# Four of the weight units per attention stage are reduced by GpSimd, and TensorE only adds their partitions

## The reference

```
# hybrid_layer, run for l = 0 and l = 1
shift, scale, gate = split(c @ w_ada[l] + b_ada[l], 3)       # [1024] @ [1024, 3072]
u = x * (1 + scale) + shift
h = split_cols(u @ w_in[l])
... attention of three kinds (dsa, fox, nsa: compressed, selected, window) ...
y = (mix * silu(h["gate"])) @ w_out[l]
x = layer_norm(ALPHA * x + (1 + gate) * y, ln_g[l], ln_b[l])

# second_block, once
mod   = silu(c_2)     @ w_mod_2 + b_mod_2                    # [1024] @ [1024, 6144]
mod_c = silu(c_ctx_2) @ w_mod_2 + b_mod_2
sh1, sc1, gt1, sh2, sc2, gt2       = split(mod, 6)
csh1, csc1, cgt1, csh2, csc2, cgt2 = split(mod_c, 6)
... gated delta net on latents and context, then 16 experts, uses of the context end early ...
```

## Time and profile before

| | us |
|---|---|
| three runs: lowest, median, highest | 1301.52, 1306.74, 1315.82 |
| the profiled execution, whole | 1302.77 |
| its span in the trace | 1301.0 |
| TensorE busy | 1073.4 (83%) |
| VectorE busy | 430.2 (33%) |
| ScalarE busy | 225.9 (17%) |
| GpSimd busy | 64.3 (5%) |

### The profile page before, as it was taken

The page is one execution under the profiler, slowest core; times in us unless marked ns, Lnnn a source line. Parts: engine busy times, 40 slices in busy tenths (PEclk is TensorE's granted clock), DMA queues, the critical chain, the costliest instruction groups (busy, mean ns, idle before and its releaser), DMA issues.

```text
span 1301.0 us, 17728 instructions
## 1 busy us (share of the span) xinstructions
PE 1073.4 (83%) x7534; PEld 576.8 (44%) x7534; DVE 430.2 (33%) x1039; ACT 225.9 (17%) x550; POOL 64.3 (5%) x73
## 2 busy tenths in 40 slices
PE   2899999999999999999998879677766666666675
PEld 0344674444576448975777865322211111111111
DVE  0124656333765545354256673311000000000001
ACT  0102125111213423532121232100000000000001
POOL 1001000000100000002203400000000000000000
PEclk9899999999999999899988999798887878888879
DMA  9663337553346962113110016189999999999996
GB/s 375 288 265 123 130 129 283 185 197 130 129 146 258 428 241 109 65 57 139 66 66 3 3 66 228 63 363 431 429 428 430 430 430 429 430 430 429 431 429 260
DMA packets 24558, 323.66 MB, mean 249 GB/s; under 512 B 2736, under 2 KB 2736, under 8 KB 5152
## 3 DMA queue, kind: packets, MB, share of 16 engines
q1 hardware_dynamic: 22448, 314.18, 58.9%
q0 software_dynamic: 2032, 8.35, 1.9%
HBM read 321.47 MB, written 1.05 MB: 248 GB/s over the span
## 4 chain that ended last, share of the span: by engine, by line
PE 58%; DMA 29%; DVE 7%; issue 3%; ACT 1%; another core or an unknown queue 1%; SPq 0%; POOL 0%; DVEq 0%; ACTq 0%; POOLq 0%
PE banks L602 48%; DMA Vt_to_O<-in_stream 14%; DMA ring<-in_stream 10%; PE banks L613 3%; DMA QKT<-in_stream 2%; DMA zuv_to_Kt<-in_stream 2%; PE banks L2039 1%; PE banks L826 1%; DVE Vt_to_O L2309 1%; PE banks L847 1%; PE banks L812 1%; PE banks L809 1%; PE banks L713 1%; DVE probs L1163 1%
## 5 line engine op out<-in xcount | busy, mean ns | idle before, releaser
L602 PE MATMUL banks<-ring,uT 128*128 128x512 f32 (+1 forms) x512 | 225.0, 595 | 6.3 <-DVE uT L1022 3.7
L602 PEld LDWEIGHTS banks<-ring,uT 128*128 128x128 f32 x512 | 96.4, 192 | 119.7 <-issue 114.0
L602 PE MATMUL banks<-ring,scr 128*32 128x512 f32 (+1 forms) x656 | 112.8, 696 | 38.8 <-DMA ring<-in_stream 38.5
L602 PE MATMUL banks<-ring,UWK 128*32 128x512 f32 (+1 forms) x368 | 91.4, 786 | 15.1 <-DMA ring<-in_stream 10.5
L2506 DVE SCALAR_TENSOR_TENSOR UWK<-UWK,banks 128x256 f32<-128x256 f32 x16 | 6.7, 422 | 285.5 <-ACT UWK L2750 285.5
L602 PE MATMUL banks<-scr 64*64 64x64 f32 (+2 forms) x2048 | 82.4, 234 | 6.3 <-DVE scr L2357 5.2
L602 PEld LDWEIGHTS banks<-scr 64*64 64x64 f32 (+1 forms) x2048 | 79.0, 144 | 12.3 <-DVE scr L2357 5.8
L602 PEld LDWEIGHTS banks<-ring,scr 128*32 128x32 f32 (+1 forms) x656 | 29.7, 127 | 114.7 <-DMA ring<-in_stream 60.5
L2039 PE MATMUL banks<-UWK 128*128 128x512 f32 x128 | 58.7, 602 | 25.6 <-DVE UWK L2516 25.6
L613 PE MATMUL banks<-ring,KC 128*32 128x512 f32 x384 | 53.1, 683 | 27.1 <-DMA ring<-in_stream 27.1
L2750 ACT ACTIVATE UWK<-banks 128x256 f32<-128x256 f32 x16 | 6.1, 383 | 397.7 <-PE banks L602 397.7
(11 more groups left out here) (361 smaller groups left out, 1191.7 us busy)
## 6 DMA issues: line engine op xcount, KB each, us to landing
ring<-in_stream SPq DMA_DIRECT2D x106, 2048.0 KB, 17.3
QKT<-in_stream SPq DMA_DIRECT2D x14, 2048.0 KB, 30.8
Vt_to_O<-in_stream SPq DMA_DIRECT2D x14, 2048.0 KB, 30.8
zuv_to_Kt<-in_stream SPq DMA_DIRECT2D x14, 2048.0 KB, 30.1
w<-in_w POOLq DMA_DIRECT2D x2, 1024.0 KB, 9.6
probs<-in_rows POOLq DMA_DIRECT2D x4, 512.0 KB, 4.7
const<-in_consts SPq DMA_DIRECT2D x1, 1215.0 KB, 5.6
resid<-in_x SPq DMA_DIRECT2D x1, 1024.0 KB, 24.2
```

The lines of the kernel that those rows point to most:

```text
L602: return pe.matmul(o, a, b, start=start, stop=stop)
```

## The change

In each of the two attention stages GpSimd takes four units: of layer 0's stage the units 0 to 3 of the six of `w_ada`, of layer 1's stage the units 8 to 11 of the twelve of `w_mod_2`. For each of the eight chunks of a unit it multiplies the 512 columns, in place in the ring, by the vector's value of each partition (tensor_scalar) and adds the chunks up in an accumulator of 128x512 that lies in `w1`, whose first use in the layer is over. TensorE keeps the other units (2 and 8), and at m = 11 the new `pe_parts` adds the partitions of the four accumulators by four matmuls with a window of ones (`onewin`), before it begins the output product. VectorE writes that window in `v_window` and `v_mod_window`; its copy of bank 7 waits for `part_mm`. The order of the stream is changed so that GpSimd's units lie between TensorE's.

```
+POOLED = {0: range(4), 1: range(8, 12)}
...
-            for cg in range(6):
+            for cg in (0, 4, 1, 5, 2, 3):
                 cols("w_ada", l + 1, cg * 512, 512, "ada_mm", l + 1, cg)
         else:
-            for cg in range(12):
+            for cg in (8, 0, 1, 9, 2, 3, 10, 4, 5, 11, 6, 7):
                 cols("w_mod_2", 0, cg * 512, 512, "mod_mm", cg)
...
+        onewin = kc_flat[:, 944:944 + 63]
...
+        acc = w1[:, :, :, :].rearrange("p v a n -> p (v a n)").rearrange("p (i n) -> p i n", i=4)
...
+        def pool_units(pool, l):
+
+            pool.wait_ge(*at("cmp1", l, 0))
+            pool.wait_ge(*at("cmp1", l, 1))
+            pool.wait_ge(*at(*(("mod_mm",) if l else ("ada_mm", 1)), "window"))
+            win, col = (modwin, MOD_AT) if l else (adawin, ADA_AT)
+            for i, n in enumerate(POOLED[l]):
+                w = take(pool, k=units.index(unit_event(l, n)))
+                o = acc[:, i % 4, :]
+                for k in range(DCH):
+                    pool.tensor_scalar(w[:, k, :], w[:, k, :], win[:, k, col:col + 1], None, ALU.mult).then_inc(*tick("pool_step"))
+                    pool.wait_ge(*last("pool_step"))
+                    if k:
+                        ins = pool.tensor_tensor(o, w[:, 0, :] if k == 1 else o, w[:, k, :], ALU.add)
...
         def pool_layer(pool, l):
             if l:
                 pool.wait_ge(*at("cmp1", l - 1, 0))
                 pool.wait_ge(*at("cmp1", l - 1, 1))
+                pool.wait_ge(*at("part_mm", l - 1))
             pool.dma_start(w1[:, :, :, :], A["w1"][l].rearrange("p (v a n) -> p v a n", v=2, a=LPAIR)).then_inc(*tick("cmp_in", by=16))
...
+            pool_units(pool, l)
             pool.wait_ge(*at("probT_mm", l, NPAIR - 1, 1))
...
+        def pe_parts(pe, l):
+
+            for j, n in enumerate(POOLED[l]):
+                pe.wait_ge(*at(*unit_event(l, n)))
+                r = 31 - (2 * n if l else n)
+                ins = pe.matmul(bank[7][32 * j:32 * j + 32, :], onewin[:, r:r + 32], acc[:, j, :], start=False, stop=True)
+            ins.then_inc(*tick("bank7_filled", "part_mm", l))
...
                     if l + 1 < DEPTH:
-                        for n in range(6 * (m - 2) // 9, 6 * (m - 1) // 9):
-                            pe_ada(pe, l + 1, n)
+                        if m in (3, 6):
+                            pe_ada(pe, l + 1, 3 + m // 3)
                     else:
-                        for n in range(12 * (m - 2) // 9, 12 * (m - 1) // 9):
+                        for n in range(8 * (m - 2) // 9, 8 * (m - 1) // 9):
                             pe_mod_rows(pe, n)
                 if m == NPAIR:
+                    pe_parts(pe, l)
                     w_out += [take(pe)]
                     pe_y(pe, l, 0, 0, w_out, range(0, 5))
...
+            dve.memset(onewin, 0.0).then_inc(*tick("vector_step"))
             dve.memset(adawin, 0.0).then_inc(*tick("vector_step"))
+            dve.wait_ge(*last("vector_step"))
+            dve.memset(onewin[:, 31:32], 1.0).then_inc(*tick("vector_step"))
...
         def v_ada_rows(dve, l):
-            dve.wait_ge(*at("ada_mm", l, 5 if l else 3))
+            dve.wait_ge(*(at("part_mm", 0) if l else at("ada_mm", 0, 3)))
```

More of the change, by code:

```diff
@@ L137, in constants, with pooled @@
     return c
+POOLED = {0: range(4), 1: range(8, 12)}
+def pooled(*event):
+    return (event[0:2] == ("ada_mm", 1) and event[2] in POOLED[0]) or (event[0] == "mod_mm" and event[1] in POOLED[1])
 def unit_order():
@@ L481, in build, with take @@
         unit_at = [0]
-        def take(pe, n=512):
-            k = unit_at[0]
-            unit_at[0] += 1
+        def take(pe, n=512, k=None):
+            if k is None:
+                while pooled(*units[unit_at[0]]):
+                    unit_at[0] += 1
+                k = unit_at[0]
+                unit_at[0] += 1
             pe.wait_ge(K.sem(f"arrived{slot[k]}"), 16 * use[k])
@@ L561, in pool_chunks, with unit_event @@
                     pool.tensor_tensor(v[:, t], v[:, t], RW("gm"), ALU.mult).then_inc(*tick("pool_step", "v_rows", t))
+        def unit_event(l, n):
+            return ("mod_mm", n) if l else ("ada_mm", 1, n)
+        def pool_units(pool, l):
[11 more added lines that the diff above has]
+                        ins = pool.tensor_tensor(o, w[:, 0, :] if k == 1 else o, w[:, k, :], ALU.add)
+                        if k < DCH - 1:
+                            ins.then_inc(*tick("pool_step"))
+                        else:
+                            ins.then_inc(*tick("pool_step", *unit_event(l, n)))
         def pool_layer(pool, l):
@@ L625, in pe_ada @@
             else:
-                first, final, b = 0, 5, 7
+                first, final, b = 4, None, 7
             pe_rows(pe, ("ada_mm", l), adawin, ADA_AT, 1, n, first, final, b)
         def pe_mod_rows(pe, n):
-            pe_rows(pe, ("mod_mm",), modwin, MOD_AT, 2, n, 0, 11, 7)
+            pe_rows(pe, ("mod_mm",), modwin, MOD_AT, 2, n, 0, None, 7)
+        def pe_parts(pe, l):
[4 more added lines that the diff above has]
+            ins.then_inc(*tick("bank7_filled", "part_mm", l))
+            K.events["use", "part_mm", l] = K.events["use", "mod_mm", 0] if l else K.events["use", "ada_mm", 1, 4]
         def pe_ada_columns(pe, l):
@@ L2047, in v_mod_rows @@
         def v_mod_rows(dve):
-            dve.wait_ge(*at("mod_mm", 11))
+            dve.wait_ge(*at("part_mm", 1))
             dve.tensor_copy(modrows[:, :], bank[7][:, :]).then_inc(*drain(7, "modrows"))
```

## The result

| | before | with the change |
|---|---|---|
| median of four runs each, us | 1304.13 | 1364.56 |
| lowest and highest, us | 1300.91, 1315.82 | 1360.40, 1367.27 |
| the profiled execution, whole, us | 1302.77 | 1367.27 |
| its span, us, and mean granted clock | 1301.0, 0.926 | 1365.5, 0.898 |

The kernel is slower by a factor of 1.044, with an interval from 1.037 to 1.052. The prediction said slower, 1357 us, from 1325 to 1392.

What follows compares the result with a forecast made beforehand. GpSimd was to become the bound of both attention stages, with TensorE waiting at pe_parts. 30.5 us in layer 0, 20.5 in layer 1 and 3 for the clock gave +54 on 1302.77, so 1357 us, range 1325 to 1392.

Steps and rivals of the forecast that it cites:

- The bound: Both attention stages: GpSimd's four units, 85 us, don't fit into 59 or 68 us, so TensorE waits at pe_parts.
- the case that I gave 0.62: Whole kernel: the forecast itself, a time from 1340 to 1370 us, chance 0.62.
- The unit: One unit on GpSimd: eight weightings of 1.50, eight waits of 0.06 and seven additions of 1.25 us make 21.2 us.
- the proportional end of my bounds: GpSimd's weighting of 512 columns: 1.58 us, scaled in proportion from 1186 ns for 384 columns; with a fixed part, 1.34.
- Contention on GpSimd: GpSimd's additions beside VectorE's port-taking operations: 5 collisions at 0.5 us make 2.5, taken as 3 us a stage.
- So adding collides and weighting doesn't: GpSimd beside VectorE: an addition pair took 3.50 instead of 2.50 us, while a tensor_scalar and VectorE hardly disturb each other.
- Contention on VectorE: Attention steps: VectorE loses perhaps 1 us a step, hidden while TensorE has to wait for GpSimd.
- My rival of the ports: VectorE's five port-taking operations a step each wait 1.4 us for a GpSimd instruction; steps 10 us, kernel 1389; chance 0.13.
- The two stages: Attention stages: the output product begins 30.5 us later in layer 0 and 20.5 us later in layer 1.
- The ring: Layer 1's stage: slots held by GpSimd delay TensorE's eighth unit (425 to 436) and eleventh (445 to 458), hidden.
- The clock: After TensorE's wait for GpSimd in each stage: slower matmuls at a lower granted clock, 1.5 us each, 3 us together.
- my signs of being wrong: Profile after: a tensor_scalar far from 1.5 us, VectorE's steps at 8 us or more, or other stages changed in length.

Runs made afterwards that it cites:

- the idle load: Kernel before the change, plus two (or four) units' arithmetic per attention stage on GpSimd, on unused w1 data, nobody waiting: 1315.71 us, 1.0099 (four: 1315.04 us, 1.0085).
- fills: Kernel before the change, plus 76 GpSimd memsets of 128x512 in w1 per attention stage, each waited for before the next: 1311.90 us, 1.0049.
- delayed load: Kernel before the change, plus two units' unused arithmetic per stage on GpSimd, begun only after VectorE's last gate tile: 1309.61 us, 1.0044.

## Why the prediction was right

**The bound.** The step on which the forecast rested, that GpSimd becomes the bound of both stages and `pe_parts` stands ahead of the output product, is shown for layer 0. GpSimd is busy for 85 of 89 us, TensorE's wait of 19.96 us ends with its last addition, and the wait goes when the chain is shortened in either of two ways, by fewer units or by fewer additions. In layer 1 the bound is nearly shared: I had put TensorE's wait for GpSimd at 10 to 15 us, and it is 2.12, so that the waits for slots that GpSimd holds reach almost as far as its own chain. The time is in the case that I gave 0.62.

**The unit.** Predicted 21.2 us, measured 22.1. The weighting took 1.56 to 1.58 us where I had taken 1.50. The proportional end of my bounds, 1.58, came out. Whether the cost is really proportional and the value per partition free, or two effects cancel, no run separates. The adding took 1.27 (1.25 predicted), the wait some 0.08 (0.06).

**Contention on GpSimd.** Predicted 3 us a stage, and this did not happen. Its longest weighting is 1720 ns and its longest adding 1387, with medians within 7 ns of the shortest. Thus 85 + 3 = 88 met the measured 88.1 us by luck, with two errors that cancel, the weighting's size and this term. "So adding collides and weighting doesn't" was wrong in both halves as to who pays: both hold VectorE up, and GpSimd hardly pays for either.

**Contention on VectorE.** Predicted 1 us a step and hidden. The four tensor_scalar took 1.7 to 3.0 us in layer 0 instead of 1.01, up to twice the predicted loss, as here in the changed kernel's VectorE:

```profile
205.67 1.70 DVE L1360 TENSOR_SCALAR probs<-probs,rin 128x128 f32<-128x128 f32 x4
...
209.40 2.79 DVE L1360 TENSOR_SCALAR probs<-probs,rin 128x128 f32<-128x128 f32 x4
```

In layer 0 it was hidden, since TensorE waits for GpSimd anyway, and GpSimd ran at its own pace. It isn't small: TensorE reached `pe_parts` at 239.19, where 7.4 us less work would have put it at about 224, and so its wait was 20 us and not 30. Without that wait some of it shows: the idle load costs 0.9 to 1.0% in two measurements. My rival of the ports, steps of 10 us and 1389 in all, is refuted. The Trainium skill (SBUF — State Buffer, Who interferes with whom) has the loser of the port pair blocked for the whole of the other's instruction. VectorE's rows agree with a loser that waits, 0.56 us more a step beside fills of 0.54 us and 0.7 to 2.0 us more beside operations of 1.27 and 1.56 us. They don't bear out my rival, in which each of the five operations of a step waits for a whole one. The short ranges of GpSimd's durations add that in this kernel the loser was nearly always the same.

**The two stages.** Layer 0: predicted GpSimd's end at 261.1 and the product at 262.1, measured 261.08 and 262.98; +30.5 against +31.3. Layer 1: +20.5 predicted, 22.8 measured from the window to the product. GpSimd begins at 421.81 and ends at 511.72, 89.9 us instead of 88, and 1.6 of it are two waits for its own units. The remaining 3.0 us between the stages came in without a new wait, at a lower granted clock: 1.0 in the output product (5.60 instead of 4.56 us), and 1.7 in one product of sixteen records, first before, then after:

```profile
337.38 7.11 PE L602 MATMUL banks<-ring,uT 128*128 128x512 f32 x16
```

```profile
369.77 8.81 PE L640 MATMUL banks<-ring,uT 128*128 128x512 f32 x16
```

The granted clock there is 1.00 before and 0.81 after. The kernel with two units' idle load has the same 8.81 us in that product, though TensorE never waits longer than 4.21 us in its layer 0.

**The ring.** The two waits of layer 1 came at the units for which I had put them, 2.95 and 10.30 us, where I had worked out 11 and 13. As predicted, a larger wait ends behind them, but by 2.12 us only. What I did not see is that they are a second limit of the idea. With two and three units, where GpSimd is waited for little or not at all, they are the largest loss.

**The clock.** I allowed 3 us for what follows the two waits. The rows right behind them show 1.0 in layer 0 and nothing in layer 1, where the output product takes 4.56 us as before. The mean granted clock fell from 0.926 to 0.898. The stages' windows have 0.81 and 0.83 instead of 0.97 and 0.99, most of it behind GpSimd's chain and free. But 7.4 us came in after both stages, where the kernel has not changed; that was one of my signs of being wrong. Windows over the stretch from the load of `grow` to GpSimd's first product of the delta net, first before:

```profile
496.93:589.75 92.82, 90.65 (x466) 77.40 (x465) 43.01 (x102) 41.05 (x88) 0.81 (x1) 0.96 0.19 69
```

then after:

```profile
554.05:651.60 97.55, 95.37 (x466) 81.07 (x465) 43.02 (x102) 41.05 (x88) 0.81 (x2) 0.91 0.19 71
```

The same 466 matmuls take 4.7 us longer, at a clock of 0.91 instead of 0.96, with no new wait of TensorE. The next stretch adds 2.9 us at 0.92 instead of 0.94, and from 740 (before) to the end nothing comes in.

The traces speak against TensorE's long waits as the cause. In the changed kernel the clock is 1.00 from 547 to 576. It falls where 64 matmuls of 128x16 begin (576.50, 519.39 before), as it does in the kernel before: over the 20 us from there it is 0.66, and 0.83 before. And the kernel with fills on GpSimd, in which TensorE never waits for GpSimd in the stages, takes the same time for the stretch:

```profile
502.15:599.70 97.55, 95.38 (x466) 81.06 (x465) 43.01 (x102) 41.04 (x88) 0.81 (x1) 0.91 0.19 71
```

In the profiled executions this stretch takes 92.8 us before and with two units, 94.5 with three, 97.6 with the change. That looks like an order by units, but either idle load has 96.0 and the fills have 97.6, and they cost the kernel 1.0 and 0.5% in all. The same kernel also moves that much by itself. Eleven executions of the kernel before on one chip go from 1298.4 us at a mean clock of 0.933 to 1311.5 at 0.919, and the four of the changed kernel from 1360.4 at 0.910 to 1367.3 at 0.898, the profiled one. So the 7.4 us are not shown to be an effect of the change; what makes the low stretches longer in one execution than in another, the runs don't settle.

**The sum.** Predicted +54, measured +64.5 in the span: +0.8 in layer 0, +3.0 between the stages, +2.3 in layer 1's stage and +7.4 behind both, less the 3 that I had allowed. That is 10.5 us, most of it clock, and the profiled execution is the slowest of the four. The medians of the runs differ by 60.4.

What wasn't tried: one GpSimd instruction that weights and adds at once, and a copy of the units into buffers outside of the ring.

## What to carry to other kernels

Before work goes to an idle engine, multiply its instructions there by the duration of the nearest row and compare that with the stretch in which it must be hidden, not with the engine's idle share: 88 us of work did not fit beside 59, at a share of 5%. Then ask what the work holds while it runs. Here it held a slot of a small ring for 22 us where its neighbours take 2, and it held up VectorE, so that half of the same work, with nobody waiting for it, still made the kernel 1% longer; that was dear in layer 0, where TensorE waits for VectorE, and in layer 1, begun a little later, free. What TensorE can save, 6.5 us a stage, is the ceiling for all of that.

## What the runs showed of the hardware

- The loss between GpSimd and VectorE was one-sided. GpSimd's operations of 128x512 stayed at 1.56 us (longest 1.72) and 1.27 us (longest 1.39), while VectorE's four in-place tensor_scalar of a step went from 1.01 us to 1.38 to 1.60 beside fills, 1.36 to 2.10 beside weighting and 1.62 to 2.99 beside weighting and adding. Where GpSimd had ended, they took 1.01 us again.
- That loss of VectorE's cost the kernel 7.0 us in layer 0's stage and 0.1 us in layer 1's, with the same delayed load beside both.
- VectorE's small product with two inputs went from 165 to 463 ns in the mean beside GpSimd's reading work, and stayed at 165 among fills. Its maxima from a bank, 128x512, took 681 ns before and 680 with the change.
- A GpSimd tensor_scalar with one input (1.56 us for 128x512) is slower than its tensor_tensor with two (1.27 us). The Trainium skill (GPSIMD Engine Reference, 3.1 Elementwise — side-by-side cycle accounting) has 769 ns for 512 elements in its best loop with one input; this operation took twice that. A fill of the same size took 537 ns.
